# Two recurrences in one stage: sums loaded two chunks ahead, and the scan's state joined before the fourth level

## What is computed

```python
def hgrn2_chunked(q, k, v, log_f):          # per chunk
        cum = jnp.cumsum(li, axis=2)
        diff = cum[:, :, :, None, :] - cum[:, :, None, :, :]
        scores = jnp.einsum('bhtd,bhsd,bhtsd->bhts', qi, ki, decay)      # decay = exp(diff), causal
        o = (jnp.einsum('bhts,bhsv->bhtv', scores, vi)
             + jnp.einsum('bhtd,bhdv->bhtv', qi * jnp.exp(cum), state))
        state = (state * jnp.exp(last[:, :, 0, :, None])
                 + jnp.einsum('bhsd,bhsv->bhdv', ki * jnp.exp(last - cum), vi))

def ssd_chunked(x, dt, A, Bm, Cm):          # per chunk
        y = jnp.einsum('btsg,btsgj,bsgjp->btgjp', cb, L, xi)             # cb = C B, L = exp(diff), causal
        y = y + jnp.einsum('btgn,bgjpn,btgj->btgjp', ci, state, jnp.exp(cum))
        state = (state * jnp.exp(last)[..., None, None]
                 + jnp.einsum('bsgn,bsgj,bsgjp->bgjpn', bi, jnp.exp(last[:, None] - cum), xi))
```

## Time and profile before

| | |
|---|---|
| time, median of 3 runs | 5129.66 us (5117.74 to 5135.55) |
| the profiled execution's own time | 5131.58 us |
| its span in the trace | 5129.9 us, mean granted TensorE clock 0.891 |
| busy over the span | PE 4116.6 (80%), DVE 2536.0 (49%), ACT 1578.4 (31%), POOL 1132.7 (22%) |
| the stage `mixers` | about 4050 to 4700 us of the span |

### The profile page before, as it was taken

One profiled execution on the slowest core, in us unless ns is written; L12 is line 12 of the kernel. 1 busy time (PEld: TensorE's weight loads), 2 busy tenths in 40 slices (PEclk: granted clock), 3 DMA queues, 4 the chain that ended last, 5 costly groups with the idle time before them and its releaser, 6 DMA issues. The chain is left out here.

```text
span 5129.9 us, 50832 instructions
## 1 busy us (share of the span) xinstructions
PE 4116.6 (80%) x19014; PEld 3246.2 (63%) x19014; DVE 2536.0 (49%) x3304; ACT 1578.4 (31%) x2582; POOL 1132.7 (22%) x911
## 2 busy tenths in 40 slices
PE   7748998677697899767769799999988356655998
PEld 1436887566466788656638578778876255544776
DVE  1444853577433594367736643410000677765554
ACT  1233102556221210256622212331112543433331
POOL 0312110111020111011102011111110155655443
PEclk9968999788898999878889899999998688887998
DMA  7423122311251312231135222231211444444543
GB/s 289 166 83 139 62 78 79 88 48 44 85 205 52 108 74 78 86 74 48 38 122 179 109 74 74 78 125 72 74 74 70 125 105 102 113 116 130 177 169 108
DMA packets 307709, 527.88 MB, mean 103 GB/s; under 512 B 26238, under 2 KB 203030, under 8 KB 288344
## 3 DMA queue, kind: packets, MB, share of 16 engines
q1 hardware_dynamic: 272362, 364.87, 23.3%
q0 software_dynamic: 35136, 160.23, 8.3%
HBM read 372.02 MB, written 153.00 MB: 102 GB/s over the span
## 5 line engine op out<-in xcount | busy, mean ns | idle before, releaser
L457 PE MATMUL in_ps<-h,in_wp 128*128 128x512 f32 x6624 | 1510.4, 390 | 18.7 <-POOL in_wp L620 18.7
L457 PEld LDWEIGHTS in_ps<-h,in_wp 128*128 128x128 f32 x6624 | 1248.1, 189 | 281.0 <-POOL in_wp L620 21.1
L1620 PE MATMUL out_ps<-out_y,out_wp 128*128 128x512 f32 x3072 | 722.9, 397 | 73.6 <-ACT out_y L1514 34.7
L1620 PEld LDWEIGHTS out_ps<-out_y,out_wp 128*128 128x128 f32 x3072 | 586.4, 191 | 209.4 <-issue 64.2
L590 DVE SCALAR_TENSOR_TENSOR cy<-cu,in_cw,cy 128x2048 f32<-128x2048 f32 x120 | 314.5, 2621 | 4.3
L1553 POOL TENSOR_TENSOR out_wp<-out_w,out_wp 128x2048 fp32r<-128x2048 f32 (+1 forms) x48 | 192.9, 4022 | 425.8 <-ACT out_wp L1503 425.8
L518 ACT ACTIVATE in_ob<-in_ps 128x2048 f32<-128x2048 f32 x37 | 69.7, 1884 | 664.3 <-PE in_ps L457 664.3
L981 DVE TENSOR_TENSOR att_pT<-att_T,att_pT 128x512 fp32r<-128x512 f32 x320 | 220.9, 691 | 97.0 <-ACT att_pT L905 96.7
L620 POOL TENSOR_TENSOR in_wp<-in_w,in_wp 128x1024 fp32r<-128x1024 f32 x75 | 201.8, 2692 | 251.5 <-ACT in_wp L468 216.3
L960 DVE CUSTOM_DVE_ANT_0 att_S<-att_S,att_mk,att_nsink 128x640 f32<-128x640 f32 x256 | 226.6, 885 | 41.2 <-PE att_S L829 39.6
L671 DVE TENSOR_TENSOR hi_wp<-hi_w,hi_wp 128x512 fp32r<-128x512 f32 x8 | 4.9, 683 | 460.6 <-ACT hi_wp L691 460.6
(11 more groups left out here) (480 smaller groups left out, 6589.8 us busy)
## 6 DMA issues: line engine op xcount, KB each, us to landing
in_w<-in_w_in SPq DMA_DIRECT2D x75, 512.0 KB, 3.6
ada_w<-in_w_ada SPq DMA_DIRECT2D x18, 2048.0 KB, 9.6
gates<-in_ob POOLq DMA_DIRECT2D x36, 1024.0 KB, 4.2
out_w<-in_w_out SPq DMA_DIRECT2D x32, 1024.0 KB, 4.9
att_qf<-q SPq DMA_DIRECT2D x64, 256.0 KB, 4.3
out_yr<-y SPq DMA_DIRECT2D x16, 1024.0 KB, 7.8
x<-out_x POOLq DMA_DIRECT2D x64, 256.0 KB, 2.5
out_yr<-y SPq DMA_DIRECT2D x32, 512.0 KB, 5.7
```

The costliest lines, as they stand in the source:

```text
L457: mm = nc.tensor.matmul(ps[:, q, c * W:(c + 1) * W], wp[:, q, i, k], h[:, j, k, c * W:(c + 1) * W], start=(n + k == 0), stop=(n == 2 and k ...
L1620: mm = nc.tensor.matmul(ps[:, u % NB, :W], wp[:, u % NW, a, k], y[:, c % 2, b, k], start=(i + k == 0), stop=(i == 2 and k == KY - 1))
```

## The change

`hload` runs one chunk further ahead. Chunk 2 is loaded before the ticks, between `eload(0)` and `uload(1)`; in an even tick SP issues `hload(c + 2)` instead of `hload(c + 1)`, and behind `uload` and `eload` instead of ahead of them. Its waits, by its argument, are one chunk later with it. On VectorE `advance` moves from the end of the tick to right behind `scale`, ahead of the fourth level; on TensorE `update` moves ahead of the fourth level's products, right behind `between`. No instruction is added or removed.

```diff
@@ sync
             bload(0)
             eload(0)
+            hload(2)
             uload(1)
             eload(1)
...
                     if c + 1 < C:
                         bload(c + 1)
                         vload(c + 1)
-                else:
-                    if c + 1 < C:
-                        hload(c + 1)
                 u = unit(T)
                 if u is not None and u + 2 < U:
                     uload(u + 2)
                     eload(u + 2)
+                if T % 2 == 0 and c + 2 < C:
+                    hload(c + 2)
@@ vector
                 hg(2)
                 if u is not None:
                     scale(u)
+                    advance(u)
                 hg(3)
                 if unit(T - 2) is not None:
                     norm(unit(T - 2))
                 if late(T) is not None:
                     hscale(late(T))
-                if u is not None:
-                    advance(u)
@@ tensor
                 if u is not None:
                     between(u)
+                    update(u)
                 if lv[3]:
                     level(*lv[3])
-                if u is not None:
-                    update(u)
```

## The result

| | before | after |
|---|---|---|
| time, median of 4 runs on the same chip | 5126.90 us (5117.74 to 5135.55) | 4973.05 us (4970.33 to 4979.71) |
| the profiled execution, its span | 5131.58, 5129.9 us | 4970.33, 4968.7 us |
| stage, first difference to the end of the last norm | 636.56 us | 485.39 us |
| mean of the thirteen chunks | 39.43 us | 28.91 us |

The ratio is 0.9702, 95% interval 0.9682 to 0.9722: faster by 3%. The forecast was 4978 in 4958 to 5015. The two profiled executions lie 161.2 us apart. Of this the stage gives 636.56 - 485.39 = 151.2; it also starts 9.4 us earlier (4048.18 against 4057.62), in work that the change does not touch. So the sum of the prediction, 151.7, stands against 151.2; between the medians the drop is 153.9.

The account below looks back on a forecast made before the run. The prediction took the stage as bound by VectorE in its order plus its waits. Terms -126.9 - 12.6 - 15.2 - 4 + 7 = -151.7 us took 5131.58 to 4979.9, forecast 4978 against the median; range 4958 to 5015.

Parts of the forecast that it names:

- the steady loads: VectorE's 13 waits for the running sums and companions, in thirteen chunks: all go with loads two chunks ahead, -126.9 us.
- The first wait: VectorE's first load wait, 16.03 us: the load starts 12.6 us earlier, so 3.4 remain, -12.6 us.
- That ends, but TensorE is not the bound: TensorE's 1.95 us per tick waiting for the state before the turn ends; VectorE gains only product waits, -4 us.
- the term for the loads: VectorE's waits for loads, steady and first: -126.9 and -12.6 us, 139.5 together.
- that for the state: State moved ahead of the fourth level: -15.2 us root waits, -4 product waits, +7 costs; 12.2 net.
- (d): Cost: without the stall and the tick's idle ends, GpSimd and VectorE collide a little more; part of +7 us.
- (a): Cost: fourth level's products come one update later, 1.02 to 1.91 us, covered by VectorE's two state instructions, 1.76 us.
- (b): Cost: VectorE's state addition waits for an update just issued, 0 at full clock, up to 0.2 us at half.
- (c): Cost: eighth level's pick comes 1.76 us later, TensorE's even tick behind it; 0 to some 0.5 us per chunk.
- Rival (1): Second half gives nothing, VectorE and GpSimd already at a shared floor of 29.7 us a chunk: 4990 or 4997; chance 0.24.
- (2): Loads still come late in part; half of each wait kept brings 70 us back: 5048 us; chance 0.12.
- (3): Slower: state addition waits for TensorE's update in each of 32 ticks; at 5.5 us, 5166 us; chance 0.02.

Follow-up runs that it names:

- the loads alone: Kernel before with only the SP edits, the four loads moved and asked for a chunk earlier: 4999.50 us, ratio 0.9767.
- The state alone: Kernel before with only the VectorE and TensorE edits, SP's loads in the old order: 5054.31 us, ratio 0.9879.
- the cover kernel: Changed kernel, but state addition between fourth level and norm, update behind the fourth level's products: 4965.12 us, ratio 0.9699 to the kernel before.

## Why the prediction was right, and where it was not

**The bound and the steady loads: right.** VectorE's list closed before and closes after, and all 13 waits for the loads went. SP's order costs nothing, as I had it, with 13.5 us of slack in the mean and not 18. Where I put the gain down to being asked for a chunk earlier, the place in SP's burst alone would have done. **The first wait: right in size,** 11.8 us gone of the 12.6 expected.

**The failed step is "That ends, but TensorE is not the bound", with the waits for the root and for the products taken at their size of before, 13.4 and 5.5 us.** Those were sizes beside a 9.8 us stall in each chunk, which let the other engines catch up. Without it they are 27.5 and 17.1 in the same 13 chunks, and TensorE's wait for the state grows from 45.7 to 74.2. So the term for the loads was some 21 us too large (118.3 measured, 139.5 predicted) and that for the state 21 too small (32.9 behind the loads, 12.2 predicted). TensorE is not the bound, but its late turn reaches VectorE through the second pick of the odd tick, and the root came late in the same ticks. Both errors are these hidden waits, booked once as never arising and once as nothing to save; with both halves in, they cancel, since VectorE ends without waits either way. The total was right; the split was not. Had the change been the loads alone, the same working would have given a stage of 636.6 - 139.5 = 497.1 us, against 518.3. The state alone gave 66.8 and not 12.2, because the stall stands at the head of a loop that it shortens, which the working did not have.

**The costs: right in size, by a way that I had not seen.** I had +7, a part of it for (d), time beside GpSimd; VectorE's busy time rose by 7.5. But it fell by 9.8 when the stall went and rose by 17.2 when the state moved, so that the sizes agree is luck. (a) and (b) measured nothing: no wait for a fourth level's product, none for the update. (c) is the one wait left, 1.2 us for the output product in 13 chunks, 2.5 when the changed kernel ran again.

**Slips that did not matter.** The four small waits for the root, 3.0 us together, give 2.7 at nine tenths and not 2.9. A fifth of a wait kept in each chunk would add some 25 us to the upper bound and not 10. The pair of the earlier trace rows does not end together: VectorE's instruction ends at 4358.62, GpSimd's at 4358.34.

**Rival (1) half right.** The shared floor of VectorE and GpSimd is real: 8.0 us less of GpSimd is worth 4.25 a chunk. But it was not reached at 29.7. What it forecast, that the second half gives nothing, is refuted by 32.9 us. VectorE is now 0.99 busy, its time beside GpSimd included, and that bounds the stage today. **Rivals (2) and (3)** show no row: no steady wait for a load, and none of the state addition for the update in the changed kernel.

Not settled: whether one order of VectorE and GpSimd is better than another by more than a third of a us a chunk. The lengths depend on which pairs meet, and I moved those only by chance.

## What to carry to other kernels

A wait's size in a profile holds only beside the other waits: when a long stall goes, take the shorter waits behind it, and the waits of the engines that it let catch up, at a larger size, and put the two halves of a change into the sum together. A load that is issued behind a wait on the same queue makes a loop with the work that it feeds. Before loading further ahead, look at what else that wait releases: putting the urgent load first in the burst took all the steady waits here, behind the same wait. Where an engine is full, ask how much of its busy time is standing beside another before taking work off it.

## What was not expected of the hardware

Taking work off VectorE can leave its busy time the same. The two differences taken away were worth some 0.8 us a chunk at 0.41 each, and 1.4 as they ran in the cover kernel, yet VectorE's busy time rose from 363.1 to 366.3 us in the 13 chunks. The negation of 128x4 values took 741 ns in the mean, 149 at least and 1033 at most over the stage. A pair from the changed kernel shows how coarse this is: a difference that starts 0.08 us behind a GpSimd product ends 0.28 us behind it and takes 1.48 us, against 0.41 alone:

```profile
4317.09 1.28 POOL L2052 TENSOR_TENSOR mix_L<-mix_L,mix_CB 128x512 f32<-128x512 f32 x1
4317.17 1.48 DVE L2273 TENSOR_TENSOR mix_X<-mix_cum 128x256 f32<-128x256 f32 x1
```

And an update more on TensorE, which VectorE does not wait for, made the chunk 0.2 us shorter in its one execution, presumably since other pairs meet; no run tests that.
